# A hybrid decoder step: four of the twelve chunks of the delta rule's convolution move from VectorE to GpSimd

## What is computed

```python
def causal_conv(x, buf, w, b=None):
    T = x.shape[1]
    ext = jnp.concatenate([buf.astype(x.dtype), x], axis=1)
    y = ext[:, 0:T] * w[0]
    for j in range(1, CONV_W):
        y = y + ext[:, j:j + T] * w[j]
    ...
    return y, ext[:, -(CONV_W - 1):]

    qkv, dn_buf_new = causal_conv(dn_qkv, dn_buf, dn_conv_w)
    qkv = jax.nn.silu(qkv.astype(f32))
    ...
    dq = l2norm(dq.reshape(B, T, DN_HEADS, DN_HD)) * (DN_HD ** -0.5)
    dk = l2norm(dk.reshape(B, T, DN_HEADS, DN_HD))
```

## Time and profile before

| | us |
|---|---|
| median of 3 runs | 2072.61 (2072.47 to 2074.95) |
| the profiled execution: time | 2070.01 |
| the profiled execution: span of the trace | 2068.2 |
| TensorE busy | 1971.1 |
| VectorE busy | 756.0 |
| ScalarE busy | 567.7 |
| GpSimd busy | 80.5 |

### The profile page before, as it was taken

One profiled execution on the slowest core, in us unless ns is written; L12 is line 12 of the kernel. 1 busy time (PEld: TensorE's weight loads), 2 busy tenths in 40 slices (PEclk: granted clock), 3 DMA queues, 4 the chain that ended last, 5 costly groups with the idle time before them and its releaser, 6 DMA issues.

```text
span 2068.2 us, 28883 instructions
## 1 busy us (share of the span) xinstructions
PE 1971.1 (95%) x11470; PEld 1408.3 (68%) x11470; DVE 756.0 (37%) x1866; ACT 567.7 (27%) x1203; POOL 80.5 (4%) x116
## 2 busy tenths in 40 slices
PE   6999899997999999999999898999979999999999
PEld 5777678785765577777467676787857555677763
DVE  2457342413444434311134663433134454433110
ACT  4132412013346511100322333120152564211000
POOL 0000201001010000000000011010101000000000
PEclk9999999998999999999999999999989999999999
DMA  6212210112411136335042141010133111553401
GB/s 233 80 61 61 66 42 21 42 47 85 132 53 31 37 99 198 107 106 166 0 162 66 41 107 41 22 42 22 47 118 120 32 31 42 154 173 103 150 39 46
DMA packets 182494, 166.78 MB, mean 81 GB/s; under 512 B 48273, under 2 KB 173635, under 8 KB 181847
## 3 DMA queue, kind: packets, MB, share of 16 engines
q1 hardware_dynamic: 178806, 147.93, 23.7%
q0 software_dynamic: 3552, 17.00, 2.2%
HBM read 151.44 MB, written 21.71 MB: 84 GB/s over the span
## 4 chain that ended last, share of the span: by engine, by line
PE 90%; DVE 4%; ACT 4%; issue 2%; DMA 0%; SPq 0%; ACTq 0%; DVEq 0%
PE PS L827 60%; PE PS L767 6%; PE PS L1197 2%; PE PS L1210 2%; PE PS L1006 2%; PE PS L1024 2%; PE PS L1276 1%; PE PS L1026 1%; PE PS L1266 1%; PE PS L1095 1%; PE PS L1143 1%; PE PS L936 1%; PE PS L909 1%; PE PS L1117 1%; PE PS L1350 1%
## 5 line engine op out<-in xcount | busy, mean ns | idle before, releaser
L827 PE MATMUL PS<-hT,ring 128*128 128x288 f32 x3968 | 1090.2, 416 | 29.2 <-ACT arena L1438 8.8
L827 PEld LDWEIGHTS PS<-hT,ring 128*128 128x128 f32 x3968 | 730.7, 193 | 240.6 <-issue 24.4
L827 PE MATMUL PS<-zs,owr 128*128 128x288 f32 x768 | 211.7, 409 | 0.0
L827 PEld LDWEIGHTS PS<-zs,owr 128*128 128x128 f32 x768 | 141.5, 190 | 40.5 <-issue 4.6
L767 PE MATMUL PS<-con,arena 128*128 128x128 f32 (+5 forms) x934 | 142.9, 277 | 15.6 <-DMA arena<-in_nsa_k_norm 12.2
L767 PEld LDWEIGHTS PS<-con,arena 128*128 128x128 f32 (+5 forms) x934 | 107.2, 138 | 72.8 <-issue 42.2
L827 PE MATMUL PS<-arena 128*128 128x512 f32 (+1 forms) x320 | 124.8, 593 | 2.1 <-issue 2.1
L1456 ACT ACTIVATE sg<-PS 128x288 f32<-128x288 f32 x96 | 38.8, 404 | 292.7 <-PE PS L827 292.7
L1778 DVE SCALAR_TENSOR_TENSOR mpr<-sg,PS 128x288 f32<-128x288 f32 x64 | 29.1, 454 | 208.7 <-PE PS L827 206.1
L1738 DVE SCALAR_TENSOR_TENSOR arena<-arena,par 128x512 f32<-128x512 f32 x192 | 99.5, 518 | 6.8
L827 PEld LDWEIGHTS PS<-arena 128*128 128x128 f32 (+1 forms) x320 | 52.7, 179 | 71.1 <-issue 70.9
(11 more groups left out here) (291 smaller groups left out, 1872.1 us busy)
## 6 DMA issues: line engine op xcount, KB each, us to landing
ring<-in_w_in SPq DMA_DIRECT2D x54, 1024.0 KB, 5.3
arena<-in_cache_nsa_kv SPq DMA_DIRECT2D x128, 192.0 KB, 2.6
ring<-in_w_in SPq DMA_DIRECT2D x32, 256.0 KB, 3.7
arena<-in_state_nsa_win SPq DMA_DIRECT2D x32, 256.0 KB, 3.2
arena<-in_cache_nsa_kv SPq DMA_DIRECT2D x128, 64.0 KB, 1.9
arena<-in_w_out SPq DMA_DIRECT2D x4, 2048.0 KB, 10.3
out_win_sample<-in_state_nsa_win POOLq DMA_DIRECT2D x2, 4032.0 KB, 23.1
arena<-in_x_prompt SPq DMA_DIRECT2D x8, 512.0 KB, 8.6
```

The lines of the kernel that those rows point to most:

```text
L827: ins = mm(to, w, x, start=start, stop=stop, skip_group_check=True)
```

## The change

Chunks 2, 5, 8 and 11 are convolved by GpSimd, in a loop that is put behind its DRAM copy. On GpSimd each tap after the first is a multiplication into a scratch row `tap` and an addition, for the prompt and the sample part apart, with `link` between all of them. VectorE keeps the other eight chunks and runs `mix(3)` where `mix(2)` stood, ahead of the scan; behind the scan come 4, 6, 7, 9 and 10. A new semaphore `conv_p` counts GpSimd's chunks, `tail_p` its saved tails; whoever waited for `conv_ok` now waits for one or both. Semaphores are saved elsewhere: tiles 2, 3 and 4 of x share `x_in2`, and the delta rule's old state shares `lrow_in`.

```diff
+def by_vector(c):
+    return c + 1 - (c + 1) // EXTN
...
-                sp.dma_start(xr[k], dram["x_prompt"][0, k * P:(k + 1) * P, :]).then_inc(s[f"x_in{k}"], 16)
+                sp.dma_start(xr[k], dram["x_prompt"][0, k * P:(k + 1) * P, :]).then_inc(s[f"x_in{min(k, 2)}"], 16)
...
-                sp.dma_start(xr[4][f * T_S:(f + 1) * T_S], x_s[:, f * 512:(f + 1) * 512]).then_inc(s["x_in4"], 16)
+                sp.dma_start(xr[4][f * T_S:(f + 1) * T_S], x_s[:, f * 512:(f + 1) * 512]).then_inc(s["x_in2"], 16)
...
-                sp.wait_ge(s["conv_ok"], past["conv_ok"] + 12)
+                sp.wait_ge(s["conv_ok"], past["conv_ok"] + 8)
+                sp.wait_ge(s["conv_p"], past["conv_p"] + 4)
...
+                pool.wait_ge(s["lc_in"], past["lc_in"] + 1)
+                if l:
+                    pool.wait_ge(s["xs_out"], 16 * l)
+                for c in range(2, 12, EXTN):
+                    e = dext[:, c % EXTN]
+                    es = e[:, HIST + SEQ:EXT].rearrange("p (b t) -> p b t", t=S_EXT)
+                    if c == 2:
+                        nc.gpsimd.memset(e[:, 0:HIST], 0.0)
+                    link(nc.gpsimd.tensor_copy(es[:, :, 0:HIST], dhist[:, c * 24:(c + 1) * 24].rearrange("p (b t) -> p b t", t=HIST)))
+                    pool.wait_ge(s["pa"], taken(l * N_ALL + U_DC + 2 * c + 2, "A"))
+                    nc.gpsimd.tensor_copy(cst[:, 4 + c, 0:HIST], e[:, SEQ:SEQ + HIST])
+                    ins = nc.gpsimd.tensor_copy(cst[:, 4 + c, HIST:27].rearrange("p (b t) -> p b t", t=HIST), es[:, :, DEC_SEQ:])
+                    ins.then_inc(s["tail_p"], 1)
+                    d = dc[:, c]
+                    ds = d[:, SEQ:T].rearrange("p (b t) -> p b t", t=DEC_SEQ)
+                    for j in range(CONV_W):
+                        w = prm("dconv", 12 * j + c)
+                        for k, (o, x) in enumerate(((d[:, 0:SEQ], e[:, j:j + SEQ]), (ds, es[:, :, j:j + DEC_SEQ]))):
+                            if j:
+                                part = tap[:, 0:SEQ] if k == 0 else tap[:, SEQ:T].rearrange("p (b t) -> p b t", t=DEC_SEQ)
+                                link(nc.gpsimd.tensor_scalar(part, x, w, None, ALU.mult))
+                                ins = nc.gpsimd.tensor_tensor(o, o, part, ALU.add)
+                            else:
+                                ins = nc.gpsimd.tensor_scalar(o, x, w, None, ALU.mult)
+                            if j == CONV_W - 1 and k == 1:
+                                ins.then_inc(s["conv_p"], 1)
+                            else:
+                                link(ins)
...
+                pe.wait_ge(s["tail_p"], past["tail_p"] + 4)
...
-                        act.wait_ge(s[f"x_in{k}"], 16 if k < 4 else 32)
+                        act.wait_ge(s[f"x_in{min(k, 2)}"], 16 if k < 2 else 64)
...
-                            if h == 0 and c >= EXTN:
-                                act.wait_ge(s["conv_ok"], past["conv_ok"] + c - EXTN + 1)
+                            if h == 0 and c >= EXTN and c % EXTN == 2:
+                                act.wait_ge(s["conv_p"], past["conv_p"] + c // EXTN)
+                            elif h == 0 and c >= EXTN:
+                                act.wait_ge(s["conv_ok"], past["conv_ok"] + by_vector(c - EXTN))
...
                 take_before("lo_t", 2)
-                act.wait_ge(s["conv_ok"], past["conv_ok"] + 12)
+                act.wait_ge(s["conv_ok"], past["conv_ok"] + 8)
+                act.wait_ge(s["conv_p"], past["conv_p"] + 4)
                 A(dc[:, 9:12], dc[:, 9:12], ACT.Silu).then_inc(s["silu_ok"], 1)
...
-                mix(2)
+                mix(3)
...
-                for c in range(3, 12):
+                for c in (4, 6, 7, 9, 10):
                     mix(c)
```

More of the change, by code:

```diff
@@ L142 @@
 A_HEAD = {"wsm": (26668, 8 * NSM), "prow": (26924, P),
-          "lrow": (11424, D_RNN), "drow": (9888, 3 * DN_W), "dhist": (16128, 12 * DEC_BATCH * HIST),
+          "lrow": (11424, D_RNN), "drow": (9888, 3 * DN_W), "dhist": (16128, 12 * DEC_BATCH * HIST), "tap": (16416, T),
           "dext": (X0, EXTN * EXT), "rowl": (27052, D_RNN), "rowh": (27052 + D_RNN, D_RNN)}
@@ L275 @@
 LAYER_SEMS = """
-x_in0 x_in1 x_in2 x_in3 x_in4 par_in lrow_in w_in0 w_in1 ow_in0 ow_in1 par_t ssq_ok x_ps xn_ok x_t sq_ok ms_ok rstd_ok h_ok pj pa pv lam_ok lh_t u_ok lgp
+x_in0 x_in1 x_in2 par_in lrow_in w_in0 w_in1 ow_in0 ow_in1 par_t ssq_ok x_ps xn_ok x_t sq_ok ms_ok rstd_ok h_ok pj pa pv lam_ok lh_t u_ok lgp
 lg at_ok lt_ok lq_ok lru_ok lc_ok lc_in lo_t lo_ok gt_t gt_ok gs_ok nq_y nq_sw nq_r qk_ok kt_t kt_e vc_mm
@@ L292 @@
     s_sc=4, s_pv=4, s_cm=4, s_ce=4, s_cn=4, s_im=4, s_wc=4, s_m=4, s_mw=4, s_wm=4, s_sm=4, s_p=4, s_pw=4, s_tr=8,
[L293 to L297, removed]
+    s_tb=4, s_ta=4, s_mix=4, s_or=4, s_ot=4, s_z=8, dh_t=1, conv_ok=8, conv_p=4, tail_p=4, silu_ok=5, dc_ok=1,
+    sp_abs=2, sp_exp=3, gb_ok=1, n_ok=8, s0_in=128, p_z=5, p_y=5, p_g=20, p_e=5, p_x=5, p_s=5, p_d=5, p_k=15, p_b=5,
+    i_w=31, i_wm=31, i_x=31, i_xm=31, f_mm=5, f_u=4, f_v=4, f_w=5, m_mm=3, u_mm=4, f_m=3, q_w=3, q_s=4, q_n=3, q_oe=4,
+    b_gl=4, b_pe=7, b_so=1, b_vt=1, b_vn=1, b_vm=4, b_sn=4, dn_ok=1, mg_ok=32, small_in=96, sm_in=32, ln_ok=19,
+    wo_in=32, st_ok=1, kvo_ok=1,)
 def hybrid_trunk(nc, dram, out):
@@ L392, in hybrid_trunk @@
         pcT = zarea("pcT")[0:KV * NCB]
+        tap = area(A_HEAD, "tap")
         dext = area(A_HEAD, "dext").rearrange("p (c t) -> p c t", c=EXTN)
@@ L522, in states_and_gates @@
                     .then_inc(s["lrow_in"], 16)
-                sp.dma_start(drow, at_layer("state_dn_conv", l).rearrange("a b k c -> (a b k) c")).then_inc(s["dr_in"], 16)
+                sp.dma_start(drow, at_layer("state_dn_conv", l).rearrange("a b k c -> (a b k) c")).then_inc(s["lrow_in"], 16)
                 for k, name in enumerate(("dn_A_log", "dn_dt_bias")):
@@ L674, in _ @@
         def _(pool):
+            link = chained(pool, s["p_chain"])
             pool.memset(wab[:], 0.0).then_inc(s["zero"], 1)
@@ L882, in _ @@
                 dense_to(u0 + U_H0)
-                pe.wait_ge(s["lrow_in"], past["lrow_in"] + 32)
+                pe.wait_ge(s["lrow_in"], past["lrow_in"] + 48)
                 pe.wait_ge(s["x_ps"], past["x_ps"] + 1)
@@ L888, in _ @@
                 ins.then_inc(s["lh_t"], 1)
-                pe.wait_ge(s["dr_in"], past["dr_in"] + 16)
                 for c in range(12):
@@ L1485, in _ @@
                 take_to(u0 + U_DC + 18)
-                act.wait_ge(s["conv_ok"], past["conv_ok"] + 6)
+                act.wait_ge(s["conv_ok"], past["conv_ok"] + 4)
+                act.wait_ge(s["conv_p"], past["conv_p"] + 2)
                 A(dc[:, 0:6], dc[:, 0:6], ACT.Silu).then_inc(s["silu_ok"], 1)
                 take_to(u0 + U_Q)
-                act.wait_ge(s["conv_ok"], past["conv_ok"] + 9)
+                act.wait_ge(s["conv_ok"], past["conv_ok"] + 6)
+                act.wait_ge(s["conv_p"], past["conv_p"] + 3)
                 A(dc[:, 6:9], dc[:, 6:9], ACT.Silu).then_inc(s["silu_ok"], 1)
                 take_before("lo_t", 2)
-                act.wait_ge(s["conv_ok"], past["conv_ok"] + 12)
+                act.wait_ge(s["conv_ok"], past["conv_ok"] + 8)
+                act.wait_ge(s["conv_p"], past["conv_p"] + 4)
                 A(dc[:, 9:12], dc[:, 9:12], ACT.Silu).then_inc(s["silu_ok"], 1)
@@ L1818, in _ @@
                     dve.wait_ge(s["xs_out"], 16 * l)
-                V.memset(dext[:, :, 0:HIST], 0.0)
+                V.memset(dext[:, 0:2, 0:HIST], 0.0)
                 take_to(u0 + U_LZ)
```

12 lines of the change are left out of this document (6 added, 6 removed).

## The result

The changed kernel is **slower**, by 0.4%: 2082.45 us (median of 6 runs, 2078.85 to 2085.58) against 2074.18 for the kernel before (6 runs, 2072.47 to 2076.52); the ratio is 1.0040, interval 1.0024 to 1.0055, so 8.3 us are lost. The forecast of 5.95 won is 14.2 from that, and 2082.45 is outside the range given. The six times stand in two groups, 2078.85 to 2080.18 and 2084.73 to 2085.58; the profiled execution (2084.73) belongs to the upper one, and the experiments come back to what divides them. Its span is 2082.9, 14.7 more than before.

A forecast was written before the change was run, and what follows sets the result against it. TensorE, busy 95% of the span, was taken as the bound, so only its waits or clock could be won. - 2 x 3.65 + 1.35 = - 5.95 gave 2064.1, on the median's scale 2066.7 us; range 2061.5 to 2075.5.

The forecast's parts named there:

- slower rival: GpSimd's chained instructions cost more, up to 16.2 us for chunk 11 ahead of the last SiLU: 2079.0 us, chance 0.11.
- Step 1: Chunk 3 convolved ahead of the scan removes TensorE's 4.4 us wait; TensorE runs 6.35 us per layer ahead.
- Step 2: GpSimd's time for convolving one chunk: 11.7 us, bounds 9.5 and 16.2, against 3.29 for VectorE's six fused taps.
- Step 4: Chunk 11 on GpSimd, ahead of the last SiLU, is not hidden: 3.65 us per layer are won, not 6.35.
- 15.35 less the chunk's time: Gain per layer with chunk 11 on GpSimd: at most 6.35 us, nil at a chunk time of 15.35.
- deciding point at 14.7: Chunk time on GpSimd from which slower decides: 15.35 less half of the start's 1.35 us.
- its 1.69 for the clock: Loss per layer from TensorE's lower clock behind waits ahead of L936 grown past 6 us, charged twice.
- Step 3: Chunks 2, 5 and 8 on GpSimd are hidden: 11.7 us each fits in 19 us for chunk 2, 22 for 5 and 8.
- the second rival: GpSimd and VectorE block each other, the freed wait moves to chunks 2 and 5: 2071.9 us, chance 0.24.
- The rule cited in the prediction: VectorE instructions with two SBUF inputs and GpSimd instructions reading SBUF exclude one another for their whole length; in full, 2071.9 us.
- Step 5: Merged start semaphores make ScalarE's third square wait for both halves of x_sample: +1.35 us, once.
- Step 6: The joined lrow_in, tail copies, SP's load of S0 and GpSimd's queued output DMAs and first beta_rows cost nothing.

The follow-up runs named there:

- order alone: Kernel before, with VectorE convolving chunks 2 and 3 ahead of the scan and nothing on GpSimd: 2060.49 against 2072.56 us; repeated, 2060.86 against 2073.49.
- chunk 11 alone: Kernel before, with chunk 3 ahead of the scan, only chunk 11 convolved by GpSimd, and x tile 2 on its own semaphore: 2073.03 against 2073.49 us.
- 5, 8 and 11: Changed kernel with chunk 2 given back to VectorE; 2076.39 against 2073.49 us with x tile 2 on its own semaphore, 2078.86 against 2073.31 without.
- 5, 8 and 11 merged: Changed kernel with chunk 2 given back to VectorE and x tiles 2, 3 and 4 still on one semaphore: 2078.86 against 2073.31 us.
- the run with the start apart: Changed kernel with x tile 2 on its own semaphore and tiles 3 and 4 sharing another: 2082.92 against 2072.56 us for the kernel before.
- the other two kernels: Changed kernel with x tile 2 on its own semaphore, 2082.92 us; changed kernel with chunk 11 given back to VectorE, 2068.37; both against 2072.56.
- the merged start alone: Kernel before, with only x tiles 2, 3 and 4 put on one semaphore: 2075.45 against 2072.56 us.
- the work for nobody: Chunk 3 ahead of the scan, VectorE convolving all twelve chunks, GpSimd doing four chunks' instructions on constants, results unused: 2060.14 against 2073.31 us.

## Why the prediction was wrong

What each part costs, each as a difference of two runs, taken against the kernel before of its own job, and what the prediction's steps gave for it:

| part | runs | measured | predicted |
|---|---|---|---|
| chunk 3 ahead of the scan | order alone | -12.1, -12.6 | -12.7 |
| chunk 11 on GpSimd | chunk 11 alone, less order | +12.2 | +5.4 |
| chunks 5 and 8 too | 5, 8 and 11, less 11 | +3.4 | 0 |
| the merged start | 5, 8 and 11 merged, less apart | +2.6 (alone 2.9) | +1.35 |
| chunk 2 too | the change, less 5, 8 and 11 | +2.7 | 0 |

From the second -12.6 the sum is 8.3; it must be, as each row starts where the one above it ends. By the intervals of its two runs each row is uncertain by 2.6 to 3.7 us. The first two rows are far outside that and the third just outside. The merged start has a run of its own. Chunk 2's 2.7 isn't clear of noise by the medians; for it stand the wait of 6.06 us and the two groups.

The forecast missed by 14.2 us: 6.8 by chunk 11, 6.1 by chunks 2, 5 and 8, which were to cost nothing, and 1.3 by the start. The rivals were priced one at a time, each with the rest of the forecast in place. What came was a slower GpSimd, blocking and a dearer start together. The range ended at 2075.5, below the 2079.0 of the prediction's own slower rival.

**Step 1 held.** Order alone won what two times 6.35 promised, the slower clock behind the old wait among it. The profiled layer 0 alone shows 4.7, since the clock there was full behind the earlier 3.27 us wait in the kernel before and is not in order alone; layer 1 shows 6.4.

**Step 2 failed, mainly in one term.** A multiply of 512 columns was taken as 0.95 (bounds 0.83 to 0.98) and takes 1.56: 4 x 0.61 = 2.4 us. The add was 1.03 and is 1.27, 0.7 for three; the small multiplies are 0.44 and not 0.55. In sum 14.3 instead of 11.7. The error was in how one row was read. Both ends of the slope were means of several multiplies: 128 columns at 0.585 and 64 at 0.545. But the four of 64 columns began beside a product on VectorE, as did the four that took 2.85 us, and only the first of them was held up (views of the kernel before: the timeline, then GpSimd's groups at 345.6 and at 346.8 us):

```profile
345.54 0.69 DVE L1675 TENSOR_TENSOR arena<-arena 128x512 f32<-128x512 f32 x1 [2.05 <-PE PS L973]
...
L708 POOL TENSOR_SCALAR arena<-con,gtok 64x64 f32<-64x64 f32 x1 | 0.9, 938 | 3.1 <-PE PS L973 3.1
...
L708 POOL TENSOR_SCALAR arena<-con,gtok 64x64 f32<-64x64 f32 x1 | 0.4, 436 | 0.0
```

An undisturbed one took 0.436, as 64 columns on 128 partitions do (0.44). With 0.600 for an undisturbed 128 columns, the slope is 0.164/64 = 2.6 ns a column and 512 columns come to 1.58: the price was in the trace. The blocking that the prediction named was inside the mean from which it took 0.5 as fixed (it is 0.28). The mean of 634 ns, from which it took the floor of a wait, has such multiplies in it too. The other end of the range, a copy (1.04 for 1024 columns), is another operation. The two agreed, and the range between them was mistaken for a bound. Another row that held against it was the add's, at 1.9 ns a column.

**Step 4's mechanism held, its result fell with step 2.** The gain was to be 15.35 less the chunk's time. Counted to the SiLU's start the chunk took 14.6 us, which leaves 0.75 per layer of step 1's 6.35; the run with chunk 11 alone shows 6.35 - 5.7 = 0.65. The SiLU to the third group was 10.2 (10.1 predicted), and the 7.8 us stayed whole. Of the new waits ahead of the sums the first came at 3.4 us instead of 0.7; one ahead of the third group shows in the run with the start apart (1.70 in layer 0), while in the change slower matmuls take its place. The slower rival had its deciding point at 14.7, so the chunk alone would have led to about no change; and its 1.69 for the clock is seen in part: behind the 3.42 us in layer 0 the granted clock is 0.50 from 224 to 228 us, eight records take 3.85 instead of 2.10, and 0.9 of that reaches the third group.

**Step 3 failed.** Chunk 5 was to fit in 22 us and chunk 2 in 19. By itself a chunk of 14.3 still fits both, so it is the blocking that made them late, the second rival; its sign, a wait of TensorE between 148 and 172, came with the 6.06 us. Chunk 2 took 26.5 us in the profiled layer 0 and 21.9 in layer 1, chunk 5 16.2 and 22.8. In the medians the rival's loss was near: 2 x 2.6 = 5.2 us, where chunks 2, 5 and 8 cost 3.4 + 2.7. Its working was not, as it charged every instruction alike, with half or a whole short VectorE instruction, and had chunk 2 late by at most 1.6. What counts is which one is met: the product of 2.56 us and the scan of 4.96 hold up even a small instruction for their whole length. In TensorE's time it is 0.4 to 0.7 us per layer behind chunk 5, and behind chunk 2 either 0.5 to 0.9 or 6.1, as the last taps come ahead of product and scan or not. That is the best reading of the two groups: the kernels without chunk 2 on GpSimd show one band each (11 and 11 runs), those with it two (6, 9 and 12 runs). A run that moves only this race wasn't made, and the sizes leave a rest: the waits differ by 5.2 us, the means of the groups by 5.6 in the change, but by 8.6 and 9.0 in the other two kernels (the 2072.96 left out). Only one execution of an upper group has a trace, so whether there both layers are late, or the clock adds to it, stays open.

The rule cited in the prediction had the right size, and the row beside it did not. Here the trace shows 4.92 us for a 64-column add that meets the scan, against 0.32 alone; the Trainium skill (SBUF — State Buffer, Who interferes with whom) says that whichever issues first holds the shared port pair for its whole instruction, and the other is blocked. The 0.51 us read from four multiplies came from a short product, of 0.69 us.

**Step 5 was half.** The third square is 2.80 late (11.33 for 8.53), where 1.35 was forecast, and the merged start alone cost 2.9. The issues start where they did (the last at 3.7), but the loads land later than in rows 10. The summary of the line that issues them, in the kernel after:

```profile
DMA to landing us min/median/max: 6.6/7.1/7.5
```

3.7 + 7.5 = 11.2, where 9.9 was taken. The term was mis-sized because one execution's landing was used as if it were fixed; in the run with the merged start alone the longest is 8.2. The 8.53 was one execution's too, the earliest of nine traces without the merged semaphore, in which the third square begins at 8.5 to 10.2 us (mean 9.4); in the four with it, at 10.5 to 12.0 (mean 11.3). What delays the loads wasn't looked into.

**Step 6 held**, as far as runs show: no new wait of TensorE comes from the tail copies, S0 or GpSimd's outputs.

## What to carry to other kernels

Before work is moved to a slower engine, ask what the late item needs: here chunk 3 only had to stand elsewhere in VectorE's own order, and that alone gives 2060.5, 12 us better than the kernel before and 22 better than the change (across two jobs). An engine that is 36% busy is not short of time. An item at the end of a dependent chain (chunk 11) pays the slower engine's full latency, so it is the last one to move. A price for an instruction wants the same operation at two widths, each taken from single instructions that ran undisturbed: a mean can hide one that was held up. Where there is none, the range has to reach to the slowest kin, or the price is measured first. And rivals that don't exclude each other have to be added up as well.

## What the runs showed of the hardware that was not expected

- A GpSimd multiply by a per-partition scalar costs more per column (2.5 ns) than an add of two tensors (2.1).
- A copy of 3 columns on GpSimd took 2.22 us at 132.21, and 0.18 at 208.26 with VectorE idle.
- The holding up goes both ways: VectorE's product of 2304 columns took 3.37 us instead of 2.56 where GpSimd's add had begun 0.3 us ahead of it.
- VectorE's fused taps are slowed beside GpSimd's adds and multiplies: 3.29 us for six became 4.40 here and 4.80 beside the work for nobody.
- Behind waits of 3.3 to 3.5 us TensorE's clock falls in some places and not in others: behind the wait ahead of the first sum, eight records take 2.10 us at full clock, 3.85 in the changed kernel's layer 0 (granted clock 0.50, the level of 1.2 GHz) and 2.97 in its layer 1 behind the same 3.42 us. Before, 112 records behind the same 3.27 took 27.43 in layer 0 and 29.11 in layer 1. This is one reason why single executions differ by some us, and why the table of parts above rests on medians.
